# Where a modulation row is summed, stored and followed by the norm's affine rows

## What is computed

```python
for l in range(2):
    x = layer_norm(ALPHA * x + swiglu_half(x, ffn1_w1[l], ffn1_w3[l], ffn1_w2[l]), ln1_g[l], ln1_b[l])
    h = x @ w_in[l]
    ...                                     # three mixers over h: spatial gating, delta rule, linear attention
    x = layer_norm(ALPHA * x + mix, ln2_g[l], ln2_b[l])
    x = layer_norm(ALPHA * x + swiglu_half(x, ffn2_w1[l], ffn2_w3[l], ffn2_w2[l]), ln3_g[l], ln3_b[l])
# swiglu_half(x) = 0.5 * ((silu(x @ w1) * (x @ w3)) @ w2), w1 and w3 1024 x 2816, w2 2816 x 1024
mod = silu(c) @ w_ada + b_ada               # 1 x 6144: shift1, scale1, gate1, shift2, scale2, gate2
...                                         # attention with mod's first half, then 32 experts (top 4) with the other
```

## Time and profile before

| What | Value |
|---|---|
| median of three runs | 2359.45 us |
| the profiled execution, its time | 2362.47 us |
| the profiled execution, its span | 2360.8 us |
| TensorE busy | 2249.0 us, 95% of the span |
| VectorE, ScalarE, GpSimd busy | 43%, 26%, 7% |
| DMA | 633.59 MB, mean 268 GB/s |
| mean granted TensorE clock | 0.996 |

### The profile page before, as it was taken

The page is one execution under the profiler, slowest core; times in us unless marked ns, Lnnn a source line. Parts: engine busy times, 40 slices in busy tenths (PEclk is TensorE's granted clock), DMA queues, the critical chain, the costliest instruction groups (busy, mean ns, idle before and its releaser), DMA issues. The chain is left out here.

```text
span 2360.8 us, 32162 instructions
## 1 busy us (share of the span) xinstructions
PE 2249.0 (95%) x12837; PEld 1409.7 (60%) x12838; DVE 1024.1 (43%) x1488; ACT 605.1 (26%) x816; POOL 171.5 (7%) x192
## 2 busy tenths in 40 slices
PE   7999989999999998999999999999999999999998
PEld 6886875788788776668877654444333333333333
DVE  5553573665475437557548642222222222222121
ACT  4432331543443322244436510000000000000000
POOL 4100020000000001000000000110000000000000
PEclk9999999999999999999999999999999999999999
DMA  8862311686297251149625558999999999999996
GB/s 277 286 242 81 111 73 53 244 280 227 73 321 257 71 166 73 38 161 321 231 87 158 219 223 342 417 418 418 418 418 418 418 418 418 418 417 418 418 418 277
DMA packets 231951, 633.59 MB, mean 268 GB/s; under 512 B 32472, under 2 KB 128744, under 8 KB 199056
## 3 DMA queue, kind: packets, MB, share of 16 engines
q1 hardware_dynamic: 231856, 632.24, 70.7%
HBM read 631.12 MB, written 1.07 MB: 268 GB/s over the span
## 5 line engine op out<-in xcount | busy, mean ns | idle before, releaser
L382 PE MATMUL banks<-ffn_room 128*128 128x512 f32 x1920 | 454.4, 392 | 0.0
L382 PEld LDWEIGHTS banks<-ffn_room 128*128 128x128 f32 x1920 | 357.5, 188 | 73.5
L508 DVE TENSOR_TENSOR ffn_room<-memory,ffn_room 128x2048 fp32r<-128x2048 f32 x124 | 280.6, 2291 | 94.2 <-ACT ffn_room L461 94.2
L2771 DVE TENSOR_TENSOR attend_words<-banks,memory 64x512 f32<-64x512 f32 x64 | 44.2, 691 | 550.7 <-PE banks L2618 550.2
L461 ACT CAST ffn_room<-memory 128x2048 fp32r<-128x2048 f32 x124 | 232.6, 1907 | 77.1 <-PE banks L413 60.9
L413 PE MATMUL banks<-ffn_room 128*128 128x512 f32 x1056 | 247.1, 390 | 0.0
L2618 PE MATMUL banks<-attend_later,attend_words 128*64 128x512 f32 x1000 | 233.3, 601 | 14.1 <-DMA attend_later<-in_w_gate_up 12.3
L413 PEld LDWEIGHTS banks<-ffn_room 128*128 128x128 f32 x1056 | 197.9, 188 | 44.4 <-issue 3.5
L2634 PE MATMUL banks<-memory,attend_words 128*64 128x512 f32 x1008 | 223.4, 595 | 0.0
L2618 PE MATMUL banks<-memory,attend_words 128*64 128x512 f32 x776 | 181.5, 603 | 13.1 <-DMA memory<-in_w_gate_up 12.4
L2618 PEld LDWEIGHTS banks<-attend_later,attend_words 128*64 128x64 f32 x1000 | 67.0, 137 | 154.5 <-issue 102.9
(11 more groups left out here) (429 smaller groups left out, 2350.3 us busy)
## 6 DMA issues: line engine op xcount, KB each, us to landing
memory<-in_ffn_w SPq DMA_DIRECT2D x132, 1024.0 KB, 7.5
memory<-in_w_down SPq DMA_DIRECT2D x126, 1024.0 KB, 24.5
attend_later<-in_w_gate_up SPq DMA_DIRECT2D x125, 1024.0 KB, 20.6
memory<-in_w_gate_up SPq DMA_DIRECT2D x97, 1024.0 KB, 17.7
attend_words<-in_w_gate_up SPq DMA_DIRECT2D x33, 1024.0 KB, 23.7
memory<-in_w_in SPq DMA_DIRECT2D x32, 1024.0 KB, 5.7
memory<-in_w_ada SPq DMA_DIRECT2D x32, 768.0 KB, 8.2
memory<-in_w_out SPq DMA_DIRECT2D x12, 1024.0 KB, 5.2
```

The source lines that it names most:

```text
L382: m = nc.tensor.matmul(psum[:, GU + tt, :], x_parts[:, xp, k, tt * P:tt * P + P], rows, start=(n == 0), stop=(n == 3 * KD - 1))
L508: tt_op(b, chip.ring[:, chip.slot(base + i), :], a.bitcast(F32), ALU.subtract).then_inc(chip.used, 1)
L2771: m = tt_op(room.gate[halves[h], :], psum[halves[h], GATE_BANK, :], room.bias[halves[h], h * HALF:h * HALF + HALF], ALU.add)
```

## The change

The accumulator moves from `chip.xT` to `chip.norm_gb`, the place of the norm's rows. Those are therefore loaded in the phase after (`take_over`), where `finish_x` uses them. `sum_ada` moves from the last step to the place between the two blocks' transposes, in place of five dummy matmuls. It writes three rows of one bank: the stationary operand is a window of a 5-column constant `pick`, so that each third of the columns lands in its own row. VectorE takes the three rows at the start of the next phase (`take_mod`), SyncE stores them there and waits for the store before it loads the norm's rows. In the last step 6 of the 12 products held over from step 9 move ahead of `down` (`kept_back`). The `w_ada` tiles come two steps later (steps 2 to 9, not 0 to 7), and the clearing of the accumulator waits for `finish_x`.

```diff
+MOD_BANK = 7
...
+        self.pick = w.take(5)
...
+        self.mod_rows = self.norm_gb[0:3, 1, 512:1024]
...
-        if ft < ADA_ROWS:
-            order.append(("ada", ft))
+        if ADA_FIRST <= ft < ADA_FIRST + ADA_ROWS:       # ADA_FIRST = 2
+            order.append(("ada", ft - ADA_FIRST))
...
+def take_over(chip, s, sp, rows, mod):
+    if mod is not None:
+        sp.wait_ge(s["mod_row"], 1)
+        sp.dma_start(mod.rearrange("a (r n) -> (a r) n", r=3), chip.mod_rows).then_inc(s["mod_stored"], 16)
+        sp.wait_ge(s["mod_stored"], 16)
+    g, b, l = rows
+    for i, v in enumerate((g, b)):
+        sp.dma_start(chip.norm_gb[:, i, :], v[l:l + 1, :].to_broadcast([P, chip.D])).then_inc(s["norm_gb"], 16)
+
+def take_mod(chip, s):
+    chip.nc.vector.tensor_copy(chip.mod_rows, chip.psum[0:3, MOD_BANK, :]).then_inc(s["mod_row"], 1)
...
 def finish_x(chip, s, dve, chain):
     gb = chip.norm_gb
+    dve.wait_ge(s["norm_gb"], 32)
...
 # post_norm
     def tensor(pe):
-        fill(chip, free_bank, waits[0])
         for tt in range(2):
             if tt:
-                fill(chip, free_bank, waits[1])
+                between(pe)
...
 # ffn_phase
-    ada_acc = chip.xT.rearrange("p k t -> p (k t)")[:, 0:ADA_BLOCK]
+    ada_acc = chip.norm_gb.rearrange("p s d -> p (s d)")[:, 0:ADA_BLOCK]
...
+    def sum_ada(pe):
+        pe.wait_ge(chip.used, base + load_ada(ADA_ROWS - 1) + 1)
+        for i in range(3):
+            nc.tensor.matmul(psum[0:3, MOD_BANK, :], chip.pick[:, 2 - i:5 - i], ada_acc[:, i * 512:i * 512 + 512],
+                             start=(i == 0), stop=(i == 2))
...
+            if rows_before:
+                take_over(chip, s, sp, rows_before, mod_before)
             sp.wait_ge(s["gu1"], 1)
-            chip.issue(sp, loads, base + RING, base + RING + 2)
+            chip.issue(sp, loads, base + RING, base + RING + 8)
             sp.wait_ge(s["acc_zero"], 1)
             sp.dma_start(ada_acc[0:1, :], b_ada).then_inc(s["acc_bias"], 16)
...
-            sp.wait_ge(s["mod_row"], 1)
-            sp.dma_start(mod_row, ada_acc[0:1, :]).then_inc(s["mod_stored"], 16)
-            sp.wait_ge(s["mod_stored"], 16)
...
+            def kept_back(ft):
+                for c in range(C):
+                    for hp, wp in PASSES:
+                        product(ft, 1, c, hp, wp, 0)
...
-                            for step in ((ft,), (ft - 1, ft))[tt]:
+                            for step in (ft - 1, ft) if tt and h else (ft,):
...
                 else:
-                    sum_ada()
+                    kept_back(ft - 1)
                 down(ft)
...
-            pool.wait_ge(s["gu1"], 1)
+            if rows_before:
+                pool.wait_ge(s["x_final"], NT)
             nc.gpsimd.memset(ada_acc, 0.0).then_inc(s["acc_zero"], 1)
...
-            take_mod()
-            act.wait_ge(s["mod_stored"], 16)
             n_scalar(act)
...
 # mix_phase: SyncE after its small loads; VectorE first of all
+            take_over(chip, s, sp_, rows_before, mod_before)
+            take_mod(chip, s)
             finish_x(chip, s, dve, chain)
 # attend_phase: SyncE ahead of its small loads; VectorE behind its first three operations; PSUM banks of the dummies
+            take_over(chip, s, sp, rows_before, mod_row[0:1, 3 * ADA_BLOCK:4 * ADA_BLOCK])
+            take_mod(chip, s)
+            dve.wait_ge(s["norm_gb"], 32)       # ahead of finish_rows(0)
```

More of the change, by code:

```diff
@@ L295, with ffn_phase @@
 POST_NORM = "norm_gb norm_gbT variance deviation scaling normal x_new x_turned xT_new x_final"
-def ffn_phase(chip, s, spent, l, loads, base, F, FT, gamma_beta, skip, room, b_ada, mod_row, unfinished, on_gpsimd=None, columns=()):
+def ffn_phase(chip, s, spent, l, loads, base, F, FT, gamma_beta, skip, room, b_ada, rows_before, mod_before, on_gpsimd=None, columns=()):
     nc, D, KD, NT = chip.nc, chip.D, chip.KD, chip.NT
@@ L396, in turn, with product @@
                 m.then_inc(s["turned"], 1)
[L398 to L404, removed]
+            def product(ft, tt, c, hp, wp, h):
+                rows = down_rows[:, ft % 2, wp, :].rearrange("p (c n) -> p c n", c=C)
+                return nc.tensor.matmul(psum[:, 2 * tt + h, :], hidden_parts[:, ft % 2, hp, tt, c, :],
+                                        rows[:, c, h * 512:h * 512 + 512],
+                                        start=(ft == 0 and c == 0 and (hp, wp) == PASSES[0]),
+                                        stop=(ft == STEPS - 1 and c == C - 1 and (hp, wp) == PASSES[2]))
+            def kept_back(ft):
+                for c in range(C):
+                    for hp, wp in PASSES:
+                        product(ft, 1, c, hp, wp, 0)
             def down(ft):
@@ L409, in down @@
                 last = ft == STEPS - 1
[L411 to L414, removed]
-                                            start=(ft == 0 and c == 0 and (hp, wp) == PASSES[0]),
-                                            stop=(ft == STEPS - 1 and c == C - 1 and (hp, wp) == PASSES[2]))
                 if last:
@@ L548, in _ @@
                     low(i)
-                if ft == 0:
-                    ada(ft)
-                if ft == 1 and unfinished:
+                if ft == 1 and rows_before:
                     finish_x(chip, s, dve, chain)
             n_vector(dve, chain)
-FFN = "columns acc_zero acc_bias mod_mm mod_row mod_stored pchain gu0 gu1 x_lead lead hidden hidden_lead hidden_low turned gate down chain " + POST_NORM
+FFN = "columns acc_zero acc_bias mod_row mod_stored pchain gu0 gu1 x_lead lead hidden hidden_lead hidden_low turned gate down chain " + POST_NORM
 def masks(chip, pool, chain):
@@ L709, in head_of, with mix_phase @@
     return 2 * (e % 4) + e // 4
[L712 removed]
+def mix_phase(chip, s, spent, l, loads, base, par, gamma_beta, skip, room, rows_before, mod_before):
     nc, D, KD, NT = chip.nc, chip.D, chip.KD, chip.NT
@@ L1560 @@
 ADA_RING = 2
-ATTEND = ("chain pchain small norm2 mod ones sq_act sq_dve ss rms_all ht x_lead x_low lead low split_used evac count ln_in ln_out "
+ATTEND = ("mod_row mod_stored norm_gb chain pchain small norm2 mod ones sq_act sq_dve ss rms_all ht x_lead x_low lead low split_used evac count ln_in ln_out "
           "lam lam_e counted x_final sq_heads h_ss h_rms normed heads_turned q_T k_T score scored t_max exp w w_turned wT pv o "
@@ L1864, in _ @@
             row_sums()
-            fill(chip, 6, 8)
+            fill(chip, 3, 8)
             for u in range(12):
@@ L2040, in _ @@
             act.wait_ge(s["ss"], 1)
-            func(room.rows_rms, psum[:, 7, 0:chip.T], ACT.Sqrt, bias=chip.eps[:, 2:3], scale=1 / D).then_inc(s["rms_all"], 1)
+            func(room.rows_rms, psum[:, 6, 0:chip.T], ACT.Sqrt, bias=chip.eps[:, 2:3], scale=1 / D).then_inc(s["rms_all"], 1)
             for k in range(4):
```

57 lines of the change are left out of this document (27 added, 30 removed).

## The result

The changed kernel takes 2348.59 us, the median of five runs (2347.55 to 2352.28), beside 2359.45 us for the kernel before (five runs, 2357.26 to 2362.44). The ratio is 0.9948, interval [0.9938, 0.9959]. In two later comparisons, on two other chips, it was 0.9942 [0.9929, 0.9956] and 0.9947 [0.9934, 0.9961]. Over five comparisons the kernel before has a mean of 2361.7 us (85 runs), over three the changed kernel has 2349.8 us (15 runs): 11.9 us, give or take about 1.1. Taken chip by chip, the means of the two kernels lie 10.1, 12.9 and 11.2 us apart, 11.4 on average, give or take about 1.3. The forecast was 9.56 us.

A forecast was written before the change was run, and what follows sets the result against it. From the statistics on, the chain through VectorE and ScalarE was taken to bound each feed-forward phase's end. Gains of 1.09 and 1.30 us make 2.39 a phase, 9.56 over four: median 2349.9 us, range 2347.5 to 2352, whole range to 2356.

The forecast's parts named there:

- Step 1: Feed-forward end: `sum_ada` leaves the place ahead of `down`, six `kept_back` products fill the wait; gain 1.09 us, bounds 0.9 and 1.2.
- Step 2: Feed-forward norm: Sqrt's table load carries no wait and runs early, so the root comes 1.30 us earlier; bounds 0 and 1.30.
- Step 3: Products, VectorE and `sum_ada` up to the phase's end: all fit, so each of four phases keeps the whole 2.39 us.
- Step 4: Phase starts: added store, later loads and `take_mod` cost nothing; up to 3 us at the attention, 2 per later feed-forward phase.
- rival 3: FFN 2 to 4: SyncE's longer queue is late and the kernel slower, 2364.9 us at 5 us of lateness; chance 0.06.
- Rival 1: Feed-forward ends: only half the gain arrives, 4.4 us by earlier products alone or 5.2 by the freed load alone; chance 0.07.
- Rival 2: Norm gaps: TensorE's clock falls behind three-column matmuls, costing 1.9 us a phase, 7.6 in all, to 2357.5 us; chance 0.09.

The follow-up runs named there:

- Experiment 2: Changed kernel without `kept_back`: all twelve held products stand behind `down`'s wait again; 2355.61 us (7 runs), ratio 0.9970.
- experiment 3: Changed kernel with `sum_ada` back ahead of `down`, five dummies between the transposes, no `kept_back`, freed table load kept; 2360.53 us, ratio 0.9993.
- Experiment 1: Changed kernel with one more, already met wait ahead of the root, so the Sqrt table load waits for the variance; 2359.98 us, ratio 0.9985.
- after_third: The changed kernel unchanged, run again in a later comparison; 2351.85 us (5 runs), ratio 0.9947.
- experiment 6: Kernel before and changed kernel with `pick`'s words, its memsets or start dummies varied, or unchanged; timed ratios 0.9997 to 1.0001 and 0.9946 to 0.9947.
- experiment 4: Kernel before with only ScalarE's wait for the stored modulation row moved from ahead of the root to ahead of the first scaling; 2362.99 us, ratio 1.0002.
- Experiment 5: Changed kernel with the sum behind both blocks' transposes in place of three dummies, nothing between the blocks; 2361.64 us (11 runs), ratio 0.9997.

## Why the prediction was right in its mechanism and wrong in its size

- **Step 1** said the products start at 200.70 and the first statistics come 1.09 us earlier. Counted from `turn`, the first aggregate ended at 206.60 - 198.59 = 8.01 before and at 203.80 - 196.91 = 6.89 now: 1.12. Experiment 2 shows `kept_back` necessary (1.38 us of this tail are lost without it), experiment 3 the place of the sum.
- **Step 2**, the table load off the chain, 1.30: the root came 9.38 us behind `turn` and comes 6.92 behind it, 2.46 with step 1's part, so 1.34. Experiment 1 holds the load and takes 1.15 us a tail back.
- **Step 3**, that the whole is kept to the phase's end, held: 11.49 to 9.04 us for the first transposes, 15.36 to 12.90 for the second, 18.33 to 15.87 for the next phase. The products ended just in time, and the sum 0.13 us ahead of the second transposes (209.68, 209.81), where the forecast had 0.29. The sum started 0.99 us behind the start of the transposes, not 0.91, and took 2.74, not 2.67.
- **Step 4**, nothing at the starts: held as to the time, not in one size. The store with its wait takes 222.15 - 217.62 = 4.5 us, where I took 2, between 1 and 3.3. It stays hidden: the affine step ends at 232.3, and from the phase's first matmul to the first product of FFN 2 it is 210.17 us in before and in after_third alike. At the attention the store costs nothing either: from the last `turn` to its first product it is 1219.82 - 1201.89 = 17.93 us, it was 1232.28 - 1211.75 = 20.53. Below are ScalarE's copies of the weights in all four feed-forward phases, first before, then after; their wait for DMA falls from 16.2 to 6.5 us, so the queue isn't later than it was and rival 3 has no ground. That this comes from the larger first issue of tiles is likely and was not tried alone. No gap opened in FFN 2 or 3 either: from the first product of FFN 2 to the last `turn` of FFN 3, with one tail between, it is 374.56 us where it was 377.41, 2.85 shorter, and the tail accounts for 2.51.

```profile
L461 ACT CAST ffn_room<-memory 128x2048 fp32r<-128x2048 f32 x124 | 232.6, 1907 | 77.1 <-PE banks L413 60.9 <-DMA memory<-in_ffn_w 16.2
```

```profile
L480 ACT CAST ffn_room<-memory 128x2048 fp32r<-128x2048 f32 x124 | 232.0, 1903 | 68.4 <-PE banks L421 61.8 <-DMA memory<-in_ffn_w 6.5
```

- **The sum.** The forecast had 4 x 2.39 = 9.56 us; the tails measured 2.46, 2.51, 2.48 and 2.60, 10.0 together. FFN 4 gave most: up to the attention's own dummies it is 18.29 us before (1211.75 to 1230.04), 15.70 after. That term was 0.4 too small. The measured time of 2348.59 is 1.3 under the forecast; the ratio puts the changed kernel at 2359.45 x 0.9948 = 2347.2, which is 0.3 below the low end of my range.
- **What failed** is thus the size of the sum, and with it the low end. The term 9.56 measured 10.0, and all that lies outside the tails was put at nothing: the step on the starts of phases allowed only for losses, and the five words of `pick`, which shift every buffer behind them, had no term at all. They gave 0.7 us in the profiles (experiment 6). With them it is 10.7 us, against 11.9 (about 1.1 either way) over all runs and 10.1, 12.9 and 11.2 chip by chip. I had set 2347.5 as the low end from the step bounds and the runs' spread, with no term for a gain outside the tails. The start of the program, 1.9 us in two profiles, is not a lasting part of it; the timings of experiment 6 leave it at 0.3 us on average, within their noise. Whether anything real remains above 10.7 us, and what it is, stays open.
- **Rival 1** had a wrong price. "With step 2 alone 5.2" us came from adding gains along one chain; experiment 4 gives nothing, since the products then end last. Step 1 alone, priced at 4.4, is nearest to experiment 1, 5.3 us by the four tails in the profile and 3.5 by the ratio.
- **Rival 2**, the clock falls behind matmuls of three columns, didn't come: the granted clock is 1.00 through the tail. But its price was real. Experiment 5 shows the fall where the engine idles 2.78 us, at 2.9 us a phase for fall and late sum together. The Trainium skill (TensorE: Matmul & The Clock Gate, What's actually happening) has the engine fall to half rate behind idle time; that experiment agrees, 0.51 behind 2.78 us of it, and so does the changed kernel, 1.00 where work fills the wait. The price I gave it, 16.0 against 14.1 us at the start of the program, came from a start whose rate did not follow the idle time ahead of it: 15.7 to 16.1 us in some profiles and 14.1 in others behind much the same 1.3 to 1.7 us.

## What to carry to other kernels

Before crediting an edit on a chain, ask what stands right behind it on the other engines: here freeing a table load was worth nothing with the sum ahead of the products and 1.15 us a phase with the sum moved. If a table load is to run ahead, look in the order of the instructions whether it carries a wait: here a second wait of the activation, already met, put the first one on the load, in each kernel that had it. Put needed TensorE work, not only dummies, into the waits of a norm: the same sum put at the end of the phase, with nothing in the wait, cost 2.9 us in FFN 1.

## What the hardware showed beyond that

- A stop of TensorE of 2.78 us between transposes was followed by half rate, in each of the four phases (experiment 5); with the sum in between the clock stayed at 1.00.
- A load of Sqrt's table took 1.28 us and ran 4.41 us ahead of its activation's wait where it carried none; where the activation had two waits, it waited for the variance first.
- Each program started at the lower rate (products of 634 ns and not 380, transposes of 421 and not 273), and the trace's first entry of the clock, at full rate, came at 15.0 to 16.7 us in eleven profiles, 17.6 in one and 20.5 to 21.2 in six. Ahead of that entry a granted clock of 1.00 says nothing. One kernel had both kinds of start, so the 1.9 us between two profiles said nothing of the timings.
- With the buffers five words further on, the feed-forward phases were 0.7 us shorter in all; FFN 4's part of it, about 0.17 us, stands in each of twelve profiles and in none of the six others.
- A 6 KB store to DRAM with the wait for it took 4.5 us on SyncE's queue, behind eleven small loads; how much of that is the loads' part was not tried.
- Single profiles of one kernel differed by up to 7.6 us, with 1.8 us at the start and short falls of TensorE's clock at changing places; so a profile shows where time is, and a count of runs how much.
